# Hybrid decoder trunk: layer 0's modulation in eight blocks of 128 features, five projection tiles accumulated over the h tiles as they come, unused modulation sums of the last layer dropped

## What is computed

```
shift, scale, gate = silu(c) W_mod + b_mod          # c: one vector of 1024, W_mod 1024 x 3072
h = RMSNorm(x) * g * (1 + scale) + shift
P = h W_in        # columns: HGRN2 q, f, i, gate; MLA c_q, c_kv, k_rope, gate; retention q, k, v, gate; 3 merge logits
y_b = mixer_b(...) * silu(gate_b)                   # b in {HGRN2, MLA, retention}
m = sum_b sigmoid(merge_b) * (y_b W_p,b)
x = x + gate * (m W_out)
```

## Time and profile before

| | |
|---|---|
| median of 3 runs | 1422.78 us (1422.21 to 1424.14) |
| profiled execution | 1425.11 us, its span 1423.3 us |
| PE busy | 1303.7 us (92%), 5886 matmuls |
| DVE, ACT, POOL busy | 765.2, 639.7, 600.1 us |
| the chain that ended last | PE 74%, DVE 14%, ACT 6%, issue 3%, DMA 1%, POOL 1% |
| first matmul of an item | at 66.7 us |

### The profile page before, as it was taken

How to read it: one execution, slowest core, us unless ns; L and a number is a source line. 1 busy time by engine, 2 the same in 40 slices (tenths; PEclk the granted TensorE clock), 3 DMA queues, 4 the chain that set the end, 5 groups by cost and what they waited for, 6 DMA issues and landing times.

```text
span 1423.3 us, 16609 instructions
## 1 busy us (share of the span) xinstructions
PE 1303.7 (92%) x5886; PEld 1033.3 (73%) x5886; DVE 765.2 (54%) x1174; ACT 639.7 (45%) x988; POOL 600.1 (42%) x756
## 2 busy tenths in 40 slices
PE   0399889999999999999978988999999999999996
PEld 0277677788777777788857777778877777778884
DVE  6867884633555524534347778463355552454433
ACT  2245554544455334444335555454445533444531
POOL 3243333465232444445534333356523244454551
PEclk9999999999999999999989999999999999999998
DMA  9121111344223233333322111135422323333321
GB/s 366 45 75 60 59 45 59 104 157 131 83 68 110 91 108 100 103 126 104 104 83 74 60 58 49 57 104 162 132 77 67 111 94 111 98 102 123 105 103 59
DMA packets 46018, 139.70 MB, mean 98 GB/s; under 512 B 5744, under 2 KB 5744, under 8 KB 45680
## 3 DMA queue, kind: packets, MB, share of 16 engines
q1 hardware_dynamic: 28656, 102.65, 21.6%
q10 hardware_dynamic: 17280, 35.99, 7.9%
HBM read 136.52 MB, written 2.10 MB: 97 GB/s over the span
## 4 chain that ended last, share of the span: by engine, by line
PE 74%; DVE 14%; ACT 6%; issue 3%; DMA 1%; POOL 1%; ACTq 0%; DVEq 0%
PE ps_st L657 20%; PE ps_st L659 20%; PE ps_st L658 20%; PE ps_o L679 4%; PE ps_s L749 2%; PE ps_s L704 1%; PE ps_s L773 1%; DVE pro_acc L1125 1%; PE ps_w L758 1%; PE ps_misc L674 1%; ACT w_hi L833 1%; DVE t L1389 1%; DMA pro_w<-w_mod_first 1%; DVE h_lo L1394 1%; DVE hg_x L1334 1%
## 5 line engine op out<-in xcount | busy, mean ns | idle before, releaser
L570 POOL TENSOR_TENSOR w_lo<-raw,w_hi 128x256 fp32r<-128x256 f32 x744 | 587.9, 821 | 774.9 <-ACT w_hi L833 774.9
L657 PE MATMUL ps_st<-h_hi,w_hi 128*128 128x512 f32 x1008 | 413.4, 410 | 1.1 <-POOL w_lo L570 1.1
L659 PE MATMUL ps_st<-h_hi,w_lo 128*128 128x512 f32 x1008 | 395.0, 392 | 0.0
L658 PE MATMUL ps_st<-h_lo,w_hi 128*128 128x512 f32 x1008 | 394.2, 391 | 0.0
L657 PEld LDWEIGHTS ps_st<-h_hi,w_hi 128*128 128x128 f32 x1008 | 190.6, 189 | 48.5 <-issue 6.4
L658 PEld LDWEIGHTS ps_st<-h_lo,w_hi 128*128 128x128 f32 x1008 | 190.8, 189 | 43.7 <-issue 6.2
L659 PEld LDWEIGHTS ps_st<-h_hi,w_lo 128*128 128x128 f32 x1008 | 190.2, 189 | 41.3
L833 ACT ACTIVATE w_hi<-raw 128x1024 fp32r<-128x1024 f32 x186 | 195.2, 1051 | 27.6 <-PE ps_st L659 27.6
L855 ACT ACTIVATE gate_t<-gate_x 128x512 f32<-128x512 f32 x80 | 50.6, 632 | 248.3 <-DVE gate_x L1184 248.3
L1184 DVE TENSOR_SCALAR gate_x<-ps_st 128x512 f32<-128x512 f32 x80 | 55.2, 690 | 186.4 <-PE ps_st L659 186.0
L1532 DVE SCALAR_TENSOR_TENSOR mod_acc<-mod_w,cond,mod_acc 128x512 f32<-128x512 f32 x84 | 75.8, 902 | 21.2 <-DMA mod_w<-w_mod 18.5
(11 more groups left out here) (233 smaller groups left out, 1987.1 us busy)
## 6 DMA issues: line engine op xcount, KB each, us to landing
raw<-w_stream SPq DMA_DIRECT2D x186, 512.0 KB, 3.4
mod_w<-w_mod ACTq DMA_DIRECT2D x96, 256.0 KB, 2.7
pro_w<-w_mod_first ACTq DMA_DIRECT2D x16, 512.0 KB, 12.5
x<-x_t SPq DMA_DIRECT2D x4, 512.0 KB, 10.2
ret_decay<-decay ACTq DMA_DIRECT2D x2, 1024.0 KB, 5.9
out_t<-o_t SPq DMA_DIRECT2D x8, 256.0 KB, 2.1
cs<-cst SPq DMA_DIRECT2D x1, 906.5 KB, 4.8
pos_i<-positions ACTq DMA_DIRECT2D x1, 256.0 KB, 7.7
```

Source lines behind the costliest of these rows:

```text
L570: ins = nc.gpsimd.tensor_tensor(w_lo[:, i % RING, r], raw[:, i % RING, r], w_hi[:, i % RING, r].bitcast(F32), ALU.subtract)
L657: nc.tensor.matmul(dst[0:m, :], wh, hi, start=(k == 0), stop=False)
L658: nc.tensor.matmul(dst[0:m, :], wh, lo, start=False, stop=False)
L659: last = nc.tensor.matmul(dst[0:m, :], wl, hi, start=False, stop=(k == nk - 1))
```

## The change

- **Prologue by blocks of 128 features.** w_mod_first is laid out as 8 blocks; block j holds, for h tile j, all 8 row tiles of its 128 shift and 128 scale columns (1 MB, a ring of 6 slots). For a block DVE adds up row tiles 0 to 5 (`DVE_TERMS`), each 256 wide, into a PSUM bank ("o"), the last of them out to pro_acc in SBUF; PE does the other two as column matmuls with the block itself as weights, and sums pro_acc with ones: 3 matmuls for the shift column, 3 for the scale column. As soon as a block is summed, h tile j is made.
- **All loads of the prologue on SP**, in the order: 141 columns of constants, x, block 0, item 0, block 1, item 1, ... (items 0 to 4 by block 4), blocks 5, 6, 7, the rest of the constants. The weights of items 3 and 4 have buffers of their own, so five items are loaded ahead of the ring. ACT issues positions, nxt and cur.
- **Five items (f0, q0, i0, cq0, g0) k-outer** over the h tiles, each in a PSUM bank of its own, item a starting at tile 0, 1, 2, 3, 5.
- **One reduction of angles and one Sin** for all tables: lanes 0 to 63 hold the retention sine and cosine, 64 to 127 MLA's; eight small DMAs spread the retention tables. The Sin, with the table load before and the one behind it, stands on ACT behind h_hi of tile 2.
- x is squared as its pieces land, into 8 tiles; POOL adds four, DVE four, PE sums both. The lower bounds (`lb`) are computed ahead of the blocks.
- **Order of items, both layers:** f0 q0 i0 cq0 g0 cq1 cq2 f1 q1 ...; after g3 cq3, cq4, cq5; hg_out of head 3 moves from behind cq4 to behind ckv1. In layer 0 levels 0 and 1 of head 0 stand behind cq1; in layer 1 hz 3 moves from behind cq0 to behind i0, and the levels of head 0 are spread one to an item.
- **The last layer** makes only sections 0 and 1 of the modulation: 32 of 48 loads and multiply-adds and 4 of 6 sums are gone there. The same output is computed.

```diff
-    for h in range(HG_HEADS):
+    if layer == 0:
+        head_0 = {("q", 0): [("hz", 0, 1)], ("i", 0): [("hz", 0, 2)], ("g", 0): [("hz", 0, 3)],
+                  ("cq", 1): [("hg_v", 0), ("hg_lv", 0, 0), ("hg_lv", 0, 1)], ("cq", 2): [("hg_lv", 0, 2), ("hg_lv", 0, 3)]}
+    else:
+        head_0 = {("q", 0): [("hz", 0, 1), ("hz", 0, 2)], ("i", 0): [("hz", 0, 3)], ("cq", 0): [("hg_lv", 0, 0), ("hg_lv", 0, 1)],
+                  ("g", 0): [("hg_v", 0), ("hg_lv", 0, 2)], ("cq", 1): [("hg_lv", 0, 3)], ("cq", 2): [("hg_lv", 0, 4)]}
...
-    item("cq", 4)
-    s += [("hg_out", h - 1)]
-    item("cq", 5)
     item("ckv", 0)
     s.append(("cq_norm",))
     item("ckv", 1)
-    s.append(("cq_rest",))
+    s += [("hg_out", h - 1), ("cq_rest",)]
...
+MOD_USED = [MOD_SECTIONS] * (DEPTH - 1) + [MOD_SECTIONS // 3]
...
+def batch_order():
+    made = [0] * len(BATCH)
+    order = []
+    for j in range(DT):
+        for a, start in enumerate(BATCH_START):
+            n = DT if j == DT - 1 else min(j + 1, made[a] + 2)
+            if j >= start:
+                order += [(a, k) for k in range(made[a], n)]
+                made[a] = n
+        order.append(None)
+    return order
...
+                def mod_columns(j):
+                    pe.wait_ge(pro_in[j % MOD_RING], 16 * (j // MOD_RING + 1))
+                    columns_of = [bank["w1"][:, what * DT + j:what * DT + j + 1] for what in range(2)]
+                    pe.wait_ge(pro_mod_done, j + 1)
+                    for what, dst in enumerate(columns_of):
+                        for k in range(DVE_TERMS, DT):
+                            nc.tensor.matmul(dst, pro_w[:, j % MOD_RING, k, what * P:(what + 1) * P], cond[:, k:k + 1],
+                                             start=(k == DVE_TERMS), stop=False)
+                        last = nc.tensor.matmul(dst, pro_acc[:, j % 2, what * P:(what + 1) * P], ones[:, 0:1],
+                                                start=False, stop=True)
+                    last.then_inc(pro_mod_sum, 1)
...
+                    mod_columns(0)
+                    mod_columns(1)
+                    j = 1
+                    for step in batch_order():
+                        if step is not None:
+                            first_step(*step)
+                        elif j + 1 < DT:
+                            j += 1
+                            mod_columns(j)
...
+                    for j in range(DT + 1):
+                        if j < DT:
+                            mod_terms(j, 0, DVE_TERMS // 2)
+                        if j >= 1:
+                            i = j - 1
+                            dve.wait_ge(pro_mod_sum, j)
+                            V.tensor_tensor(shift[:, i:i + 1], bank["w1"][:, i:i + 1], pn("b_shift")[:, i:i + 1], ALU.add)
+                            link(V.scalar_tensor_tensor(scale_g[:, i:i + 1], ...))
...
+                            V.scalar_tensor_tensor((t1, t2)[i % 2][:], x[:, i, :], scale_g[:, i:i + 1], rstd[:],
+                                                   ALU.mult, ALU.mult).then_inc(norm_t, 1)
+                        if j < DT:
+                            mod_terms(j, DVE_TERMS // 2, DVE_TERMS)
+                        if j >= 1:
+                            dve.wait_ge(norm_hi, e.at(norm_hi, j))
+                            V.scalar_tensor_tensor(h_lo[:, i, :], (t1, t2)[i % 2][:], shift[:, i:i + 1],
+                                                   h_hi[:, i, :].bitcast(F32), ALU.add, ALU.subtract).then_inc(h_ready, 1)
```

More of the change, by code:

```diff
@@ L50 @@
 PI_BELOW = 3.1415925
[L51 to L52 removed]
+MOD_RING = 6
+DVE_TERMS = 6
 TABLE_SET = "natural_log_exp_and_others"
@@ L183, in build_schedule @@
     return s
-SCHEDULE = build_schedule()
-ITEMS = [s[1:] for s in SCHEDULE if s[0] == "item"]
+SCHEDULE = [build_schedule(layer) for layer in range(DEPTH)]
+ITEMS = [s[1:] for s in SCHEDULE[0] if s[0] == "item"]
+assert all([s[1:] for s in steps if s[0] == "item"] == ITEMS for steps in SCHEDULE) and ITEMS[:len(BATCH)] == BATCH
 N_ITEMS = len(ITEMS)
@@ L206, in build_uses @@
     out = 0
-    for s in SCHEDULE:
+    for s in SCHEDULE[layer]:
         kind = s[0]
@@ L211, in build_uses @@
             use("misc", ("ssq",))
+        elif kind == "item" and layer == 0 and s[1:] in BATCH:
+            use(BATCH_BANK[BATCH.index(s[1:])], (s[1:], 0))
         elif kind == "item":
@@ L263, in add_mod_steps @@
                 continue
-            while steps and len(steps) > (total - (n - first)) * (MOD_SECTIONS * (DT + 1)) / total:
+            while steps and len(steps) > (total - (n - first)) * (MOD_USED[layer] * (DT + 1)) / total:
                 out.append(steps.pop(0))
@@ L288, in mixers_first @@
             group = [s]
-            if i < N_ITEMS:
-                out.append(("split", i + RING - 1))
+            ahead = i + len(BATCH) if layer == 0 and i < len(BATCH) else i + RING - 1
+            if i < N_ITEMS and not (layer == 0 and RING - 1 <= i < len(BATCH)):
+                out.append(("split", ahead))
         else:
@@ L294, in mixers_first @@
     return out
-MIXERS_FIRST = mixers_first()
+MIXERS_FIRST = [mixers_first(layer) for layer in range(DEPTH)]
 CUR = {}
@@ L565, in _ @@
                     n = elements_of(it)
+                    whole, hi, lo = weights(layer, i)
                     pool.wait_ge(w_hi_ready, e.at(w_hi_ready, i + 1))
@@ L628, in moving, with first_step @@
                     return h_hi[:, k, :], h_lo[:, k, :]
+                def first_step(i, k):
+                    if k == 0:
+                        pe.wait_ge(w_lo_ready, e.at(w_lo_ready, i + 1))
+                    dst = take((ITEMS[i], 0)) if k == 0 else bank[e.bank_of((ITEMS[i], 0))]
+                    hi, lo = moving("f", 0, k)
+                    _, wh, wl = weights(layer, i)
+                    wh, wl = wh[:, k * P:(k + 1) * P], wl[:, k * P:(k + 1) * P]
+                    nc.tensor.matmul(dst[:], wh, hi, start=(k == 0), stop=False)
+                    nc.tensor.matmul(dst[:], wh, lo, start=False, stop=False)
+                    last = nc.tensor.matmul(dst[:], wl, hi, start=False, stop=(k == DT - 1))
+                    if k == DT - 1:
+                        done(last, (ITEMS[i], 0))
                 def first_items():
-                    dst = [take((it, 0)) for it in ITEMS[:2]]
                     behind = 3
@@ L1381, in _ @@
+                for s in MIXERS_FIRST[layer]:
                     kind = s[0]
-                    if kind == "norm":
+                    if kind == "norm" and layer == 0:
+                        first_norm()
+                    elif kind == "norm":
                         next_rstd()
```

707 lines of the change are left out of this document (387 added, 320 removed).

## The result

The changed kernel takes 1400.17 us in the median (1396.95 to 1402.71, 4 runs) against 1422.52 us before on the same chip: ratio 0.9839, 95% interval 0.9816 to 0.9863, so 22.4 us faster. The forecast was 1405.0 us, 17.5 us faster, with 1394 to 1417 as its range. The profiled execution took 1402.71 us, its span 1400.9 us; the span of before was 1423.3 us, so the spans differ by 22.4 us too, and can be compared place by place. Run again on another chip, the same kernel gave 1398.61 us, ratio 0.9835 (0.9818 to 0.9852).

What follows compares the result with a forecast made beforehand. PE bounds it, waiting 46.3 us at the start for DVE's modulation sums. Gains 22.3, 3.6 and 1.3 less 3.4, 3.2 and 3.1 give 17.5: profiled 1425.1 becomes 1407.6, median 1405 us, range 1394 to 1417.

Steps and rivals of the forecast that it cites:

- four signs of being wrong: DVE's PSUM terms over 0.6 us, blocks waiting for DMA, clock 0.5 past 45 us, or ma2 not waiting.
- Step 1: Prologue start: DVE waits for the lower-bound parameters, third in ACT's queue, landing at 5.5 to 8.9 us; 6.5 taken.
- Rival C: Prologue blocks take longer: terms of 0.64 us, parameters at 8.9, or stretched norm steps; 1408 to 1413 us, chance 0.24.
- Step 5: Prologue loads: block 0 has landed when blocks start; each further block with its item takes 3.8 us, less than a block.
- rival D: Prologue loads: SP's single queue moves less than two did, last block lands at 58 us; about 1411 us, chance 0.05.
- Step 6: A prologue block on DVE takes 5.75 us for the first five, then 4.9; h0 at 28.9 us, h7 at 66.4.
- Step 7: PE's item steps in the prologue: behind from 57.5 us on, five items done at T = 73.2 us.
- The chain of head 0: From f0 complete to level 1, 16.5 us; level 1 can start at T + 11.7, a PE stall of 5.8 us.
- hg_out of head 3: Between ckv1 and kr it delays ma2's weight split: -3.4 us layer 0, -3.2 layer 1, -3.1 for one low clock.
- rival B: At hg_out of head 3: its delay is absorbed, no clock lost, 9.7 us come back; 1396 us, chance 0.22.
- Layer 1: Scan leaves the way to level 1, +1.3 us; four mod_sums less, +3.6; f1 to g3 0, bounds -2 and +2.
- Rival E: Prologue batch: PE's clock stays at the lower level throughout, T about 101 us; 1433 us, chance 0.07.

Runs made afterwards that it cites:

- e3: Changed kernel with the parameters cur issued ahead of the positions and nxt on ACT's queue; 1394.99 us, ratio 0.9798 to the kernel before.
- e12: e9 with DVE adding up seven of a block's eight row tiles instead of six; 1381.68 us, ratio 0.9694 to the kernel before.
- e1: Changed kernel with the column sum of head 3's hg_out in PSUM bank s0 instead of misc; 1399.09 us, ratio 0.9821 to the kernel before.
- e5: e1 with ACT's and DVE's part of head 3's hg_out moved behind ma1, PE's column sum unmoved; 1394.50 us, ratio 0.9791.
- e6: e3 with 15 unread column sums over x (9, 1 and 5) put in front of PE's work; 1394.81 us, ratio 0.9793 to the kernel before.
- e10: Changed kernel with parameters first as in e3 and the late hg_out of e5 together; 1392.09 us, ratio 0.9779 to the kernel before.
- e11: The changed kernel run again, unedited, on the same chip as others; 1398.61 us, ratio 0.9835 to the kernel before.
- e2: Changed kernel with the last layer making all 48 multiply-adds and 6 column sums again; 1403.82 us, ratio 0.9859 to the kernel before.
- e8: e5 with cq3 between cq2 and f1, and layer 0's levels of head 0 one item later; 1392.51 us, ratio 0.9788.
- e9: e10 with cq3 between cq2 and f1, and head 0's levels one item later on PE than on ACT and DVE; 1384.07 us, ratio 0.9718.
- e4: Changed kernel with 40 unread column sums over x (26, 4 and 10) put in front of PE's work; 1413.29 us, ratio 0.9924.

## Why the prediction was right, and where its steps were off

The direction, the place and the main mechanisms were right: the sums at the start were the price, DVE's terms and PE's steps set the batch, and hg_out's order costs what it costs through ACT. The gain came out 4.9 us above the forecast, and that it is no further off is luck in part, since errors cancel: 3.8 us less up to level 1, then more everywhere else: 1.8 behind level 1, where the low clock is shorter, 2.5 at hg_out, 2.2 in layer 1 ahead of c_q's norm, 1.3 behind that layer's norms, and 0.9 in small pieces. Two of my own four signs of being wrong did appear: the clock was at its lower level past 45 us, and ma2 didn't wait.

- **Step 1, the parameters.** 9.45 us where 6.5 was taken and 8.9 was the upper bound. This step failed: the bound was made from two loads alone, and cur is 13.5 KB behind 256 KB of positions on one queue while SP's loads move too. Issued first (e3) it is there by 4.32 us. Steps 2 to 4 took 12.2 us (9.45 to 21.65) for 12.4 forecast. Rival C named this case.
- **Step 5 and rival D.** DMA didn't limit: it moved 411 to 438 GB/s from 13 to 33 us with one queue, and no wait of PE or DVE on a block shows.
- **Step 6.** The term (0.52 us) and its not being stretched are as forecast; my estimate by the figure of the Trainium skill, "VectorE: DVE Perf Modes", section "The TRN2 errata", was 0.42 us, so the nearest rows were the better guide. h_lo came at 5.72 and 5.46 us for tiles 1 and 2, then PE's columns held DVE up (1.78 and 1.62 us): a part that the sum didn't have.
- **Step 7.** PE was behind from 36 us on, not from 57.5: 8 of its 40 steps ran at the low pace, up to 50.3 us, at 1.28 us each, where I had counted that pace only for the columns at the start. T was 4.6 us late, 2.75 of it from the start. In an execution with an early rise it is 74.4 us; e12 shows that PE's work is the bound.
- **The chain of head 0** took T + 10.9 instead of T + 11.7, the stall 4.8 instead of 5.8. The gain at level 1 was 18.5, not 22.3; the low clock around it was 3.4 us shorter than before by the records, and the lead grows by 1.8 us behind it.
- **hg_out of head 3.** The order as the price, ACT as the late engine and 3.9 us of stall as the size: the first two are shown by e1 and e5; the size was 2.4 and 2.2 us. What I called a wait for w_lo at ma2 was, in the changed kernel, a wait for bank misc ahead of it, of the same length; I had not looked at which bank the two sums share. The clock fell behind both of the two, where I had counted one, and for 3.4 us each, not for 6: together -7.2 us (20.3 to 17.0 and 20.8 to 18.4 in the lead table, and the 1.5 us of clock behind the second) where the sum had -9.7. That is a quarter of the way to rival B, in which nothing of it was lost.
- **Layer 1.** The scan is worth 1.6 us (forecast 1.3); the other 2 us of lead arise somewhere between the layer's sum of squares and c_q's norm, a stretch that I took as 0 with bounds of 2. I didn't test that remainder: the stretch took 195.8 us in the first trace and 193.7 to 195.9 us in the others with this order (e1 to e6, e10, e11), so it varies by as much.
- **The sums.** 4.2 us for 3.6, by e2's trace against e11's. The stretch behind c_kv's norm gained 4.9 us; the other 0.7 stay open.
- **Rival E** (the low pace through the batch) came in part: the low pace lasted 9 to 18 us after the first step, and in no trace without added sums did it last beyond 51 us. I had given it to the whole batch or to none of it.

## What to carry to other kernels

A wait moves when its cause is an in-order queue: changing the bank moved 2.4 us from one PE instruction to another, and reordering ACT removed most of it. To cover a stall, put work in front of the waiting instruction on the waiting engine alone; the same step moved on all engines lets the producer's queue eat the cover (the stall was 3.99 us in e8 and gone in e9). Before believing a clock of 1.00 at the start of a trace, look at the distance between matmuls. A small load that the first computing step needs goes ahead of the large ones on its queue.

## What the hardware did that I had not expected

- ACT loads a table set in front of the Exp of the first rstd, which neither the code nor my sum has; it is hidden, since the first t waits for PE's columns (27.70) anyway. Behind three loads of ACT's timeline work stands ready (24.49, 40.72, 42.66 us), and it starts 1.29 to 1.30 us after the load began: no drain, as in the earlier trace rows:

```profile
24.49 1.28 ACT L939 ACT_TABLE_LOAD   x1
25.78 0.63 ACT L939 ACTIVATE rstd<-rstd 128x512 f32<-128x512 f32 x1
...
42.66 1.28 ACT L1057 ACT_TABLE_LOAD   x1
43.96 1.06 ACT L931 ACTIVATE w_hi_extra<-raw_extra 128x1024 fp32r<-128x1024 f32 x1
```

- PE's first item steps run at the lower level of the clock, one matmul every 0.43 us, for 9 to 18 us in different executions, also of one program, against 7.9 us in the kernel before. Between an early and a late rise lie up to 4 us of T. The views show 1.00 there, for want of a record.
- With PE kept busy from 7 or 8 us on, the clock rose at 12.6 and 13.3 us (e6, e4). In e6 it fell to 0.50 again in a wait of 2.09 us, and in e4 2 us after one of 1.95 us, and e6's time is no shorter than e3's.
- A later low-clock stretch can hide in another's wait: in the changed kernel's trace the clock is 0.96 from 160 to 240 us, and a wait for hg_kd there is 0.47 us (188.61); in e11's, with the clock at 1.00 there, the same wait is 2.02 us (187.24). So the waits add up to less where the clock is lower, and the lead doesn't follow the sum of waits.
